# Eight input-gate tiles of the first mixer computed in quarters inside the delta-net loop

## The chip, the cores and the metric

The kernel runs on one core of a Trainium2 chip. The metric is the device time of one execution in microseconds (us); shorter is better. TensorE multiplies, VectorE (DVE), ScalarE (ACT) and GpSimd (POOL) do the elementwise work, and the SyncE queue (SP) issues the transfers of weights. All data are float32. In the trace one float32 matmul of the program leaves two TensorE records, and an identity transpose leaves one.

## The reference, cut to what matters

The program computes two transformer blocks one after the other for 256 tokens of width 1024. The part that the change touches is the end of the mixer of the first block. Two recurrent mixers (a gated delta net `dn` and an HGRN2 layer `hg`, four heads of 128 each) give one 512-wide output each. Each output goes through its own 512x1024 branch matrix, is multiplied by a sigmoid of a projection of the normed input, and the sum goes through the 1024x1024 output matrix:

```python
    def merge(parts, odn, ohg):
        br_dn = _gated_rmsnorm(odn, parts[1], dn_norm_g) @ w_br_dn
        br_hg = _gated_rmsnorm(ohg, parts[7], hg_norm_g) @ w_br_hg
        gate_dn, gate_hg = jnp.split(parts[8], 2, axis=-1)
        return (jax.nn.sigmoid(gate_dn) * br_dn + jax.nn.sigmoid(gate_hg) * br_hg) @ w_out
```

`parts[8]` is the 2048-wide gate projection of the same normed input `hx` from which all other parts come. So the gate logits do not depend on the two mixers. After this come a layer of 32 experts and the second block, which the change leaves alone.

## The kernel before, in words

**Weights.** All weights come as a stream of 1 MB blocks (`ORDER`, written by `stream_order`). SP issues them strictly in that order (`load`, L444) into a ring of slots. Up to block 48 (`EARLY`) the ring has six slots (`ring0` to `ring5`), since the other six (`ring_late`) hold intermediate values of the two mixers. Block i waits until block i-6 has been given back (`w_used`), and from block 54 on until block i-12 has. Block 54 also waits for the second `y_ready`. TensorE takes blocks in the same order (`take`) and gives them back with the increments that its matmuls carry. In the first mixer's end the blocks were: 42, 43 branch 0; 44 to 47 its gates; 48, 49 branch 1; 50 to 53 its gates; 54 to 57 the output matrix. In `merge` none of the six blocks of a branch is given back before the last gate tile of that branch (`frees` is 0 for `m2 < 3` and 5 at the first matmul of the last).

**The delta-net loop.** The delta net runs in both time directions (d = 0, 1) over four chunks s of 128 tokens. One chunk of one direction takes ten phases, and direction 1 runs four steps behind direction 0, which gives 44 steps t (`DN_SLOTS`). In phases 2 to 7 a 128x128 triangular inverse is refined: TensorE computes p (`dn_p`, four matmuls of 128 columns, one for each head), ACT copies p out of PSUM, TensorE computes x and y from it, DVE subtracts both from their operands (L1483, L1485), POOL masks a matrix for the next phase, and the next p needs DVE's and POOL's results. Phases 0, 1, 8 and 9 set up and finish a chunk. Within a step all first halves (`delta_first`) go ahead of all second halves (`delta_second`), and then comes one piece of other work (`fill_slot`): projections and transposes in steps 0 to 6, nothing from step 7 on. The four matmuls of one such product leave eight records of 128 columns.

**The end of the mixer.** After step 43 TensorE closes the output banks, ACT squares the delta-net output (`o_squares`), TensorE sums over partitions (`column_sums`), ACT takes Ln and Exp, DVE multiplies (`head_norm(1)`) and signals the second `y_ready`. Then `merge` runs eight pairs of tiles. In each pair TensorE computes a branch tile (8 matmuls of 256 columns, K = 512) and a gate tile (16 matmuls, K = 1024), ACT copies the first and takes the sigmoid of the second, and DVE multiplies, and in the second branch also adds. The last add signals `merged`, and the output product (`mix_full`, 64 matmuls) starts.

## Time and profile before

| quantity | value |
|---|---|
| time, median of 3 runs | 2779.77 us (2775.85, 2779.77, 2779.93) |
| span of the profiled execution | 2773.7 us |
| time of the profiled execution | not listed apart from its span; the lowest run is 2.2 us above the span, the median 6.1 us |
| PE busy | 2550.8 us (92%) |
| steps 7 to 43 of the delta-net loop, about | 365 to 556 us |
| from the loop's end to the second `y_ready` | 556 to 568 us |
| `merge` | 568 to 660 us |
| output product | 660 to 690 us |
| experts, loop | 745 to 1220 us |

The span runs from the first to the last instruction. A PE record's busy time has a modelled end, so the spacing from one start to the next tells how fast matmuls run. A group of the timeline view gives the start, the time it covers, the records in it and, in brackets, the idle time in front of it with the releaser. PEclk is the granted TensorE clock, where 1.0 is 2.4 GHz and 0.5 is 1.2 GHz.

### The profile page before, as it was taken

Reading aid. Unit: us, or ns where it says so; the run is one execution under the profiler, and the core shown is the slowest. Engines: PE = TensorE matmul, PEld = TensorE weight load, DVE = VectorE, ACT = ScalarE, POOL = GpSimd, SP = SyncE. Lnnn points to the kernel's source line nnn. Section 1 sums busy time; section 2 is a strip of 40 time slices with the busy share of each in tenths; the row PEclk is TensorE's granted clock in tenths of the full one; section 3 lists DMA queues with packets and bytes.
Section 4 is the critical chain, followed back from the end, with each engine's and each line's share of the span. In section 5 each row is a group of like instructions: output and inputs, shape, how many; then the busy total and the mean of one; then the engine's idle time right before and its main releaser. Section 6 shows DMA issues by size and latency. Waiting matters only on the chain.

```text
span 2773.7 us, 37722 instructions
## 1 busy us (share of the span) xinstructions
PE 2550.8 (92%) x15259; PEld 1933.4 (70%) x15264; DVE 1103.4 (40%) x2325; ACT 585.4 (21%) x1032; POOL 115.3 (4%) x98
## 2 busy tenths in 40 slices
PE   5999889989799999979999779999999997799998
PEld 2686588868456655549948468699499484586993
DVE  1455445501311111136550831366666507312665
ACT  3632422210211111121011521110100105311000
POOL 0000144300000000000000000000000000000000
PEclk8999999999999999989999889999999998799999
DMA  7126100025499999974444004344344350043340
GB/s 280 62 79 278 54 31 1 1 108 211 157 414 422 422 422 422 422 309 173 178 147 173 30 1 182 152 166 184 142 162 176 144 196 31 1 182 152 153 168 15
DMA packets 74309, 485.50 MB, mean 175 GB/s; under 512 B 7872, under 2 KB 14528, under 8 KB 16704
## 3 DMA queue, kind: packets, MB, share of 16 engines
q1 hardware_dynamic: 65808, 472.46, 42.8%
q10 hardware_dynamic: 8368, 11.14, 1.2%
q8 instruction: 98, 1.61, 0.2%
q14 instruction: 35, 0.29, 0.0%
HBM read 479.38 MB, written 4.19 MB: 174 GB/s over the span
## 4 chain that ended last, share of the span: by engine, by line
PE 82%; DVE 7%; DMA 5%; ACT 3%; issue 2%; SPq 0%; ACTq 0%; DVEq 0%; POOL 0%; POOLq 0%
PE bank L501 80%; DMA ring<-in_stream 5%; ACT arena L2010 2%; PE bank L513 2%; DVE arena L1191 1%; DVE softmax_small L1881 1%; DVE arena L1879 1%; DVE arena L1902 0%; ACT hT L2010 0%; DMA bias_scratch<-arena 0%; ACT ring_late L2010 0%; DVE arena L1449 0%; ACT L2010 0%; DVE softmax_small L1889 0%; DVE arena L1485 0%
## 5 line engine op out<-in xcount | busy, mean ns | idle before, releaser
L501 PE MATMUL bank<-arena 128*128 128x128 f32 (+4 forms) x3864 | 619.5, 318 | 67.8 <-ACT arena L2010 43.1
L501 PEld LDWEIGHTS bank<-arena 128*128 128x128 f32 (+2 forms) x3864 | 485.4, 195 | 175.5 <-issue 87.0
L501 PE MATMUL bank<-hT,ring 128*128 128x256 f32 (+2 forms) x2144 | 463.3, 374 | 8.1 <-issue 6.7
L2010 ACT ACTIVATE arena<-bank 128x512 f32<-128x512 f32 (+2 forms) x384 | 218.0, 568 | 1156.7 <-PE bank L501 1131.2
L501 PEld LDWEIGHTS bank<-hT,ring 128*128 128x128 f32 x2144 | 357.5, 193 | 97.1 <-issue 64.7
L501 PE MATMUL bank<-ring,arena 128*64 128x256 f32 (+3 forms) x2184 | 298.6, 406 | 31.3 <-DMA ring<-in_stream 29.0
L501 PE MATMUL bank<-hT,ring_late 128*128 128x256 f32 (+1 forms) x1568 | 279.4, 336 | 6.7 <-issue 6.7
L501 PEld LDWEIGHTS bank<-ring,arena 128*64 128x64 f32 (+2 forms) x2184 | 176.4, 141 | 144.7 <-issue 82.7
L501 PEld LDWEIGHTS bank<-hT,ring_late 128*128 128x128 f32 x1568 | 248.9, 193 | 31.0 <-issue 7.5
L2010 ACT ACTIVATE hT<-bank 128x256 f32<-128x256 f32 (+2 forms) x92 | 38.6, 420 | 642.4 <-PE bank L501 471.3
L501 PE MATMUL bank<-arena,ring_late 128*128 128x128 f32 (+1 forms) x1088 | 157.4, 299 | 5.1 <-DVE arena L1485 2.8
L501 PE MATMUL bank<-ring_late,hT 128*64 128x512 f32 (+2 forms) x632 | 162.0, 584 | 0.0
L1191 DVE TENSOR_TENSOR arena<-arena 128x512 f32<-128x512 f32 (+5 forms) x55 | 33.7, 615 | 321.4 <-ACT arena L2010 320.8
L501 PEld LDWEIGHTS bank<-arena,ring_late 128*128 128x128 f32 x1088 | 144.2, 193 | 12.7 <-DVE arena L1485 3.6
L513 PE MATMUL bank<-constants,arena 128*128 128x128 f32 x492 | 87.1, 325 | 58.3 <-ACT arena L2010 44.5
L501 PE MATMUL bank<-arena,ring 128*128 128x128 f32 (+1 forms) x864 | 125.0, 299 | 11.5 <-issue 8.0
L513 PEld LDWEIGHTS bank<-constants,arena 128*128 128x128 f32 x492 | 68.1, 167 | 93.1 <-issue 58.0
L1191 DVE TENSOR_TENSOR arena<-arena,bank 128x512 f32<-128x512 f32 x16 | 11.0, 688 | 303.7 <-PE bank L501 303.7
L501 PEld LDWEIGHTS bank<-arena,ring 128*128 128x128 f32 x864 | 114.1, 195 | 17.7 <-issue 12.7
L501 PEld LDWEIGHTS bank<-ring_late,hT 128*64 128x64 f32 (+1 forms) x632 | 58.1, 147 | 87.8 <-issue 85.0
L501 PE MATMUL bank<-ring_late,arena 128*64 128x256 f32 (+2 forms) x680 | 115.7, 404 | 3.2 <-DVE arena L1513 2.3
L2001 POOL TENSOR_TENSOR x_tok<-x_tok,arena 128x512 f32<-128x512 f32 x8 | 11.8, 1492 | 2207.2 <-DVE arena L1802 2207.2
(215 smaller groups left out, 2239.1 us busy)
## 6 DMA issues: line engine op xcount, KB each, us to landing
ring<-in_stream SPq DMA_DIRECT2D x248, 1024.0 KB, 8.9
ring_late<-in_stream SPq DMA_DIRECT2D x198, 1024.0 KB, 10.4
arena<-bias_scratch ACTq DMA_DIRECT2D x4, 1536.0 KB, 18.0
bias_scratch<-arena ACTq DMA_DIRECT2D x12, 256.0 KB, 2.0
constants<-in_con SPq DMA_DIRECT2D x1, 1184.0 KB, 9.3
x_tok<-in_x SPq DMA_DIRECT2D x1, 1024.0 KB, 5.3
arena<-in_ctx SPq DMA_DIRECT2D x1, 1024.0 KB, 6.8
out<-x_tok SPq DMA_DIRECT2D x2, 512.0 KB, 2.7
```

Source lines behind the costliest of these rows:

```text
L501: ins = engine.matmul(out_, lhsT, rhs, start=start, stop=stop, skip_group_check=True)
L513: ins = engine.transpose(out_, in_, ident[0:k, 0:k])
L1191: return tt(o, x, y, ALU.mult)
L1879: tt(e, src, bias2[:, m.bias], ALU.add).then_inc(*v.inc("sm_in"))
L1881: engine.tensor_reduce(stat(m, 0), e, AX.X, ALU.max).then_inc(*v.inc())
L2001: engine.tensor_tensor(x, x, ffU[j], ALU.add).then_inc(*g.inc("ff_joined"))
L2010: engine.activation(o, i, f, **kw).then_inc(*s_.inc(ev))
```

## The change

The eight gate tiles are no longer computed in `merge`. Their blocks come ahead of the branch blocks in the stream (42 to 49), those of the `hg` half first, then the branch blocks (50, 51 for `hg`; 52, 53 for `dn`), then the output matrix at 54 to 57 as before. A generator `gate_quarters` issues four matmuls of 256 columns at the end of each of the steps 7 to 38. After four quarters a tile is complete, and ACT copies it unchanged to a new place in `ring_late` (`gates1`, under slots 10 and 11) at the end of every fourth step. At steps 40 to 43 ACT takes the sigmoid of all eight tiles in place, in four passes over 1024 elements. Because `gates1` lies in slots 10 and 11, block 58 now also waits for `merged`.

After the loop the branch tiles alone are left. The branch of `hg`, whose `y_ready` is the first one, goes first. Its first tile stands ahead of `column_sums`, the other three behind it, and only then does TensorE wait for the second `y_ready`. DVE multiplies straight from PSUM with the stored gates.

```diff
--- before.py
+++ after.py
@@ -72,9 +72,8 @@
     order += qkv[0:2] + ada[0] + [("in_hg", 256 * j, "columns") for j in range(2)] + ada[1]
     order += qkv[2:3] + ada[2] + qkv[3:4] + ada[3] + qkv[4:6]
     order += [("in_z", 256 * j, "columns") for j in range(2)]
-    for b in range(2):
-        order += [(f"br{b}", 256 * j, "rows") for j in range(2)]
-        order += [("in_gate", 1024 * b + 256 * j, "columns") for j in range(4)]
+    order += [("in_gate", 1024 * b + 256 * j, "columns") for b in (1, 0) for j in range(4)]
+    order += [(f"br{b}", 256 * j, "rows") for b in (1, 0) for j in range(2)]
     order += [("out", 256 * j, "columns") for j in range(4)]
     for e in range(0, EXPERTS, 2):
         for part in ("gate", "up"):
...
@@ -343,9 +341,9 @@
         qsq, ksq = hkc, cnv
 
         a = Carve(base)
-        mrg, eg, brs = a(KT, N), [a(2, N) for _ in range(2)], [a(2, N) for _ in range(2)]
-        mtmp = a(2, N)
+        mrg, mtmp = a(KT, N), [a(2, N) for _ in range(2)]
         yx2 = a(KT, N)
+        gates1 = spare(8192, 16, N)
 
         hnZ, hnR, hnE = [None, None], [None, None], [None, None]
         hnZ[0], hnR[0], hnE[0] = hkl[0], hD[0], hX[0]
@@ -440,6 +438,8 @@
                         sp.wait_ge(sem("w_used"), i - back + 1)
                     if i == EARLY + HALF_RING:
                         sp.wait_ge(sem("y_ready"), 2)
+                    if i == EARLY + 10:
+                        sp.wait_ge(sem("merged"), 1)
                     src = A["stream"][i, :, :]
                 sp.dma_start(ring[slot][:, :], src).then_inc(sem(f"landed{slot}"), 16)
 
@@ -771,7 +771,23 @@
                     turn_tokens(v_)
                 elif t <= 6:
                     fill()
-
+                else:
+                    next(gate_pieces, None)
+
+            def gate_quarters():
+
+                for _ in range(8):
+                    w = take()[:, :].rearrange("p (m k c) -> p m k c", m=2, k=KT)
+                    t = pj_tile()
+                    for m in range(2):
+                        for k in range(KT):
+                            end = m == 1 and k == KT - 1
+                            mm(t[:, 256 * m:256 * m + 256], w[:, m, k, :], hT[:, k, LAT], start=k == 0, stop=k == KT - 1,
+                               ev="pj_full" if end else None, frees=int(end))
+                            if k % 4 == 3:
+                                yield
+
+            gate_pieces = gate_quarters()
             AB, CD = (bank[2], bank[3]), (bank[4], bank[5])
 
             def four(dst, d, f, ev=None):
@@ -865,9 +881,29 @@
                 fill_slot(t)
             clear(bank[6], stop=True)
             clear(bank[7], stop=True, ev="o_full")
-            engine.wait_ge(*pe.at("o_squared", 2))
-            column_sums([bank[3], bank[4]], flat(hnE[1]), "o_sums")
             engine.wait_ge(*pe.at("mod_read", 1))
+            engine.wait_ge(*pe.at("pj_free", state["tile"]))
+
+            def branch_tile(i, w):
+
+                if i >= 2:
+                    engine.wait_ge(*pe.at("merge_used", i - 1))
+                t = bank[i % 2]
+                for m in range(2):
+                    for k in range(4):
+                        wk = w[k // 2][:, :].rearrange("p (k c) -> p k c", k=2)
+                        c, end = 256 * (i % 4) + 128 * m, m == 1 and k == 3
+                        mm(t[:, 256 * m:256 * m + 256], wk[:, k % 2, c:c + 128], yT[1 - i // 4][:, k, :], start=k == 0,
+                           stop=k == 3, ev="branch_full" if end else None, frees=2 if end and i % 4 == 3 else 0)
+
+            for b in range(2):
+                w = [take(), take()]
+                engine.wait_ge(*pe.at("y_ready", b + 1))
+                for m2 in range(4):
+                    branch_tile(4 * b + m2, w)
+                    if b == m2 == 0:
+                        engine.wait_ge(*pe.at("o_squared", 2))
+                        column_sums([bank[3], bank[4]], flat(hnE[1]), "o_sums")
 
             def merge(branches, ys, cols, n, name="y_ready", count=None):
 
@@ -889,8 +925,6 @@
                                    stop=k == KT - 1, ev="pj_full" if k == KT - 1 and m == 1 else None,
                                    frees=0 if m2 < 3 else 5 if m == k == 0 else m == 1 and k == KT - 1)
 
-            engine.wait_ge(*pe.at("y_ready", 2))
-            merge(2, [[y[:, k, :] for k in range(4)] for y in yT], slice(NC, NC + N), 1)
             engine.wait_ge(*pe.at("merged", 1))
 
             for j in range(4):
@@ -1494,7 +1528,28 @@
                 for step in slot:
                     delta_second(step)
                 fill_slot(t)
+
+            def branch_tile(i):
+
+                engine.wait_ge(*v.at("branch_full", i + 1))
+                if i == 0:
+                    engine.wait_ge(*v.at("gates_on", 1))
+                o, g = mrg[:, 2 * (i % 4):2 * (i % 4) + 2, :], gates1[:, 2 * i:2 * i + 2, :]
+                src = bank[i % 2][:, :].rearrange("p (a b) -> p a b", a=2)
+                if i < 4:
+                    mul(o, src, g).then_inc(*v.inc("merge_used"))
+                    return
+                added = v.last()
+                mul(mtmp[i % 2], src, g).then_inc(*v.inc("merge_used"))
+                engine.wait_ge(*v.last("merge_used"))
+                engine.wait_ge(*added)
+                tt(o, o, mtmp[i % 2], ALU.add).then_inc(*v.inc("merged" if i == 7 else None))
+
+            for i in range(2):
+                branch_tile(i)
             head_norm(1, V_DNG)
+            for i in range(2, 8):
+                branch_tile(i)
 
             def merge(branches, tile, mrg, eg, brs, mtmp):
                 for b in range(branches):
@@ -1513,7 +1568,6 @@
                             tt(o, o, mtmp, ALU.add).then_inc(*v.inc("merged" if last else None))
                             engine.wait_ge(*v.last("merged" if last else None))
 
-            merge(2, TILES["merge"], mrg, eg, brs, mtmp)
             for j in range(4):
                 engine.wait_ge(*v.at("mix_full", j + 1))
                 for m in range(2):
@@ -2174,6 +2228,12 @@
                     copy_tiles([vtok[:, c].rearrange("p a b -> p (a b)") for c in range(4)])
                 elif t in (4, 6):
                     copy_tiles([hnZ[1][:, t - 4:t - 2, :]], ACT.Silu)
+                elif 7 <= t < 39 and t % 4 == 2:
+                    i = (t - 10) // 4
+                    copy_tiles([gates1[:, 2 * i:2 * i + 2, :]])
+                elif 40 <= t < 44:
+                    i = 4 * (t - 40)
+                    act(gates1[:, i:i + 4, :], gates1[:, i:i + 4, :], ACT.Sigmoid, "gates_on" if t == 43 else None)
 
             of = lambda x, d: x[:, 4 * d:4 * d + 4, :]
             ps = lambda i: bank[i][:, :].rearrange("p (a b) -> p a b", a=4)
@@ -2225,8 +2285,6 @@
                         copy_tiles([brs[i % 2]])
                         t = tile()
                         act(eg[i % 2], t[:, :].rearrange("p (a b) -> p a b", a=2), ACT.Sigmoid, "pj_free")
-
-            merge(2, 0, eg, brs)
 
             def norm(name, first, junk=None):
 
```

On TensorE, steps 14 to 18 of the loop. In the kernel before, with the segment product (`ring_late,constants`) that begins a chunk of direction 1, one transpose set (`L513`), and the x and y products behind them:

```order
L501 MATMUL bank<-ring_late,constants 128x512
L501 MATMUL bank<-arena 128x128 x16
L513 MATMUL bank<-constants,arena 128x128 x4
L501 MATMUL bank<-arena 128x128 x52
L501 MATMUL bank<-arena,ring_late 128x128 x4
L501 MATMUL bank<-ring_late,arena 128x128 x4
```

The same place in the kernel after, where `hT,ring` are the quarters:

```order
L501 MATMUL bank<-ring_late,constants 128x512
L501 MATMUL bank<-arena 128x128 x12
L501 MATMUL bank<-hT,ring 128x256 x4
L501 MATMUL bank<-arena 128x128 x4
L513 MATMUL bank<-constants,arena 128x128 x4
L501 MATMUL bank<-arena 128x128 x8
L501 MATMUL bank<-hT,ring 128x256 x4
L501 MATMUL bank<-arena 128x128 x24
L501 MATMUL bank<-hT,ring 128x256 x4
L501 MATMUL bank<-arena 128x128 x20
```

Each step now ends with four matmuls of 256 columns, just ahead of the first product of the next step. Nothing stands between the first and the second half of a step that did not stand there before.

On TensorE behind the loop, before (first rows of eight pairs):

```order
L501 MATMUL bank<-zero 128x512 x2
L501 MATMUL bank<-arena,ones 128x512 x2
L501 MATMUL bank<-arena,ring 128x256 x8
L501 MATMUL bank<-hT,ring 128x256 x16
L501 MATMUL bank<-arena,ring 128x256 x8
L501 MATMUL bank<-hT,ring 128x256 x16
```

And after, down to the output product:

```order
L501 MATMUL bank<-zero 128x512 x2
L501 MATMUL bank<-arena,ring 128x256 x8
L501 MATMUL bank<-arena,ones 128x512 x2
L501 MATMUL bank<-arena,ring 128x256 x56
L501 MATMUL bank<-arena,ring_late 128x256 x64
```

The 128 gate matmuls are gone from here, and one branch tile stands ahead of the column sums (`arena,ones`).

On ACT, the end of the loop after (copies of the delta net, sigmoids over `ring_late`, the two squares in the last row of two, then Ln and Exp):

```order
L2064 ACTIVATE arena<-bank 128x512 x2
L2064 ACT_TABLE_LOAD
L2064 ACTIVATE ring_late<-ring_late 128x1024
L2064 ACTIVATE arena<-bank 128x512
L2064 ACTIVATE ring_late<-ring_late 128x1024
L2064 ACTIVATE arena<-bank 128x512 x2
L2064 ACTIVATE ring_late<-ring_late 128x1024 x2
L2064 ACTIVATE arena<-bank 128x512 x2
L2064 ACT_TABLE_LOAD
```

The table load for the sigmoid stood behind the loop, in `merge`, and now stands at step 40; neither the copies nor the squares between it and the Ln have a load of their own.

## Rows read from the trace of the kernel before

**Rows 1.** The page: busy time by engine, with share and number of records.

```profile
PE 2550.8 (92%) x15259; PEld 1933.4 (70%) x15264; DVE 1103.4 (40%) x2325; ACT 585.4 (21%) x1032; POOL 115.3 (4%) x98
```

**Rows 2.** Windows view: loop, a slow stretch in it, and the experts.

```profile
core 0: us, PE busy (x) PEld busy (x) DVE busy (x) ACT busy (x) POOL busy (x), PEclk, DMA share, GB/s
365.00:557.00 192.00, 172.88 (x1401) 162.56 (x1401) 103.43 (x160) 48.99 (x81) 78.55 (x63) 0.99 0.02 7
412.00:414.00 2.00, 2.00 (x11) 2.00 (x11) 0.00 (x0) 0.60 (x1) 2.00 (x3) 0.50 0.00 0
...
763.00:1200.00 437.00, 434.64 (x3103) 258.59 (x3102) 58.31 (x195) 78.76 (x120) 0.00 (x0) 1.00 1.01 421
```

**Rows 3.** Waits view, 365 to 557 us: us in total, times, longest.

```profile
PE bank L501 <- ACT arena L2010: 8.7, 12, 0.9
PE bank L501 <- DVE arena L1483: 4.7, 4, 3.0
```

**Rows 4.** Timeline of PE in the loop, 364 to 560 us.

```profile
373.55 2.05 PE L501 MATMUL bank<-arena 128*128 128x128 f32 x16 [0.75 <-ACT arena L2010]
...
410.12 11.81 PE L501 MATMUL bank<-arena 128*128 128x128 f32 x88 [2.96 <-DVE arena L1483]
...
444.34 1.16 PE L501 MATMUL bank<-arena,ring_late 128*128 128x128 f32 x8 [1.02 <-DVE arena L1485]
...
464.61 10.30 PE L501 MATMUL bank<-arena 128*128 128x128 f32 x88 [1.19 <-DVE arena L1483]
...
553.90 2.05 PE L501 MATMUL bank<-arena 128*128 128x128 f32 x16 [0.78 <-DVE arena L1489]
```

**Rows 5.** Timeline of all engines behind the loop, 548 to 720 us.

```profile
556.00 0.38 PE L501 MATMUL bank<-zero 128*128 128x512 bf16 x1
...
557.76 1.98 PE L501 MATMUL bank<-arena,ones 128*128 128x512 f32 x4 [1.38 <-ACT arena L2010]
...
563.84 1.06 ACT L2010 ACTIVATE arena<-arena 128x1024 f32<-128x1024 f32 x1
...
567.76 5.55 PE L501 MATMUL bank<-arena,ring 128*128 128x256 f32 x16 [8.02 <-issue]
...
580.05 3.62 PE L501 MATMUL bank<-arena,ring 128*128 128x256 f32 x16
580.29 1.28 ACT L2010 ACT_TABLE_LOAD   x1 [6.27 <-PE bank L501]
581.59 0.60 ACT L2010 ACTIVATE arena<-bank 128x512 f32<-128x512 f32 x1
...
583.50 7.07 PE L501 MATMUL bank<-hT,ring 128*128 128x256 f32 x32
...
590.41 3.62 PE L501 MATMUL bank<-arena,ring 128*128 128x256 f32 x16
...
614.77 5.38 PE L501 MATMUL bank<-arena,ring 128*128 128x256 f32 x16 [3.48 <-DMA ring<-in_stream]
...
651.07 7.07 PE L501 MATMUL bank<-hT,ring 128*128 128x256 f32 x32
...
658.23 0.60 ACT L2010 ACTIVATE arena<-bank 128x512 f32<-128x512 f32 x1 [6.29 <-PE bank L501]
...
658.93 0.69 DVE L1191 TENSOR_TENSOR arena<-arena 128x512 f32<-128x512 f32 x1 [8.94 <-ACT arena L2010]
...
660.41 29.49 PE L501 MATMUL bank<-arena,ring_late 128*128 128x256 f32 x128 [2.27 <-DVE arena L1513]
```

**Rows 6.** Tile view of `ring`, 600 to 640 us: issue to landing of six blocks.

```profile
DMA to landing us min/median/max: 4.8/8.0/12.7
```

**Rows 7.** Timeline of ACT near the loop's end, 540 to 590 us.

```profile
543.56 0.60 ACT L2010 ACTIVATE arena<-bank 128x512 f32<-128x512 f32 x1 [3.31 <-PE bank L501]
547.46 0.60 ACT L2010 ACTIVATE arena<-bank 128x512 f32<-128x512 f32 x1 [3.31 <-PE bank L501]
```

More of the change, by code:

```diff
@@ L139 @@
             ("ada2", 1), ("hg", 2), ("ada3", 1), ("dk1", 2), ("ada4", 1), ("dk", 2), ("ada5", 1), ("dv0", 2), ("osum", 2),
-            ("qsum", 2), ("ktok", 4), ("dv", 2), ("ada", 2), ("z0", 1), ("vtok", 4), ("z", 1))
+            ("qsum", 2), ("ktok", 4), ("dv", 2), ("ada", 2), ("z0", 1), ("vtok", 4), ("z", 1), ("gates", 8))
 TILES = {name: sum(n for _, n in S1_TILES[:i + 1]) for i, (name, _) in enumerate(S1_TILES)}
-TILES["merge"] = TILES["z"]
-TILES["h2"] = TILES["merge"] + 16 + 4
+TILES["h2"] = TILES["gates"] + 4
 TILES["layers"] = TILES["h2"] + 14
```

## Prediction, made before the changed kernel ran

> **What bounds the kernel now.** I read the page first: TensorE (PE) is busy for 2550.8 us of 2773.7 [rows 1], so a change pays only where PE has less to do, waits less, or runs at the higher clock. The change touches two stretches, and I read each with the windows view, then the waits, then the timeline.
>
> The first is the delta-net loop from step 7 on, 365 to 557 us. PE is busy for 172.9 of 192 us there at a granted clock of 0.99 [rows 2], so 19.1 us are idle. The waits view splits them: 8.7 us in 12 waits on ACT (x waits for ACT's copy of p, in the middle of a step), 4.7 us in four waits on DVE's L1483 [rows 3], the rest in small ones. The timeline shows both kinds. A row such as 373.55 with 0.75 is the first kind and recurs. The wait of 2.96 at 410.12, 1.19 at 464.61 and 1.02 at 444.34 (and the same again ten steps later, at 499.55) are the second: the first products of a step wait for DVE [rows 4]. Everywhere else PE runs without a gap: 88 records in 10.30 us [rows 4].
>
> The second stretch runs from the closing of the output banks at 556.00 to the output product at 660.41, so 104.4 us [rows 5]. In it the reader is to see: 8.02 us idle while ACT and DVE turn the column sums into the second `y_ready`; eight pairs of tiles, a branch tile taking 583.50 - 580.05 = 3.45 us and a gate tile 590.41 - 583.50 = 6.91 us; 3.48 us idle for a transfer at 614.77, since the blocks of the second branch can be fetched only when the first branch gives its own back; and two branch tiles of 5.55 and 5.38 us instead of 3.62, each behind an idle time [rows 5].
>
> **What is added to the loop.** 32 quarters make up the eight gate tiles, so PE gets 8 x 6.91 = 55.3 us more work there, 1.73 us in each of 32 steps. A quarter stands at the end of a step. It can hide only in a wait of the first products of the next step, not in the 8.7 us of waits on ACT, which lie between the halves. Of the 19.1 us idle, 10.4 are not on ACT. The 2.96 wait exceeds a quarter by 1.2, and the steps 39 to 43 have no quarter; there two waits of 0.78 on DVE remain (553.90 is one [rows 4]). That leaves 7.6 us. The printed idle time leaves out the modelled tail of the record before it (a wait printed as 0.75 is 0.91 by start-to-start spacing), and summing the starts record by record I get 9.2 us for steps 8 to 38. I take 9. There is a second saving. Behind the 2.96 wait the granted clock is 0.50 [rows 2], which is 1.2 GHz, and 88 records take 11.81 us instead of 10.30 [rows 4], 1.5 more. With a quarter in that wait, and another 1.73 us before it in which DVE's work of the previous step is already under way, less than 1 us of idle is left, and I expect the fall to go. ACT's eight copies of the tiles (0.60 each) mostly end before the next p is done; in three places a transpose set of half a product's length leads the step and its copy starts some 0.1 us late, 0.3 us together. The loop costs 55.3 - 9 - 1.5 + 0.3 = 45.1 us. The bounds are 55.3 + 0.3 (nothing hidden) and 55.3 - 19.1 - 1.5 = 34.7 (all idle time filled); I stay near the record-by-record sum, since place by place it says which waits lie in front of a step.
>
> The sigmoids: four passes of 1.06 us (the Exp over 1024 elements at 563.84 is the nearest row [rows 5]) and a table load of 1.28. From the end of one copy to the next, 544.16 to 547.46, ACT has 3.3 us [rows 7]; load and pass need 2.4. The others need 1.1 each and end near 555, ahead of the squares. I cost them at nothing; uncovered they would be 4 x 1.06 + 1.28 = 5.5 us. On the load the trace has 1.28 us and the next pass starts at 581.59, 1.30 after it [rows 5]. The Trainium skill (ScalarE: Activation LUTs, What ACT_TABLE_LOAD costs) counts a drain besides and gives about 2.66 us for each switch. By that, load and pass would take 3.7 us and PE would lose 0.4 us once; by the row it loses nothing, and I go by the row.
>
> **What is left behind the loop.** The banks are closed at 556.2. Then 8 x 3.45 = 27.6 us of branch tiles and 4 x 0.43 = 1.7 us of column sums (four records of 512 columns, each twice the 0.216 of 256) bring PE to 585.5. Is PE kept going? The sums end at 556.2 + 3.45 + 1.7 = 561.4 instead of 559.5, so the second `y_ready` comes 1.9 us later, at 569.6 instead of 567.7. The fourth branch tile ends at 571.7, 2.1 us after it. DVE has multiplied tiles 0 and 1 before `head_norm(1)` and does tile 2 at 570.3, so the bank for tile 4 is free at 571.7 as well. From the last record to the output product it took 660.41 - (651.07 + 6.91) = 2.43 us; ACT's pass between them (658.23 to 658.93, 0.70) goes [rows 5], so 1.73 remain. The output product starts at 587.3 instead of 660.41, 73.1 us less: 55.3 of gate tiles moved, 9.7 of idle time around the norm (8.02 + 1.38, and drains), 1.9 + 1.8 of low clock, 3.5 of transfer wait and 0.7 of ACT.
>
> SP: blocks 54 to 57 wait for the second `y_ready` and are issued at 569.6 and in the 1.5 us behind it. Blocks fetched six at a time landed 4.8 to 12.7 us after issue [rows 6], so the last is there by 584 and the first long before, ahead of 587.3. Block 58 and all behind it wait for `merged` at 587; the first expert block is needed some 84 us later, and twelve blocks at 421 GB/s [rows 2] take 30 us. Cost nothing.
>
> **Sum.** -73.1 + 45.1 = -28.0 us. The profiled execution spans 2773.7 us, which gives 2745.7. Its own time is not listed; the median of the three runs lies 6.1 us above the span, and I keep that distance: 2751.8, rounded to 2752. The output product ran its first records at the low clock behind a wait of 2.27 us (29.49 us where 128 x 0.216 = 27.6 would do [rows 5]); I leave that 1.8 in, and it may go.
>
> **Rivals.**
> - *The waits move along.* DVE's work behind a step starts when PE's products end, and what a quarter hides may come back in the next wait. For it: the waits at 410.12 and 464.61 both name DVE's L1483 as what ended last [rows 4], and DVE's chain there is some 9 us long. Against: that chain starts from products ahead of the quarter, not from the quarter. If nothing is hidden and the slow stretch stays, the loop costs 55.6 and the sum is -17.5: 2762.
> - *More is hidden than the places allow.* POOL and DVE run ahead by 1.7 us in each step, and the waits in the middle shrink too. Then the loop costs 34.7 and the output product loses its slow start: -73.1 + 34.7 - 1.8 = -40.2: 2740. Against: the 0.75 of the wait at 373.55 is the time from PE's own p through ACT's copy, which no quarter shortens [rows 4].
> - *The output weights come late.* If blocks 54 to 57 took twice the 12.7 us, the last would land near 597 and the product would start some 6 us late and again wait between blocks; with a slow stretch behind it (1.8) about 8 us in all: 2760. Against: rows 6 and a free queue.
> - *Slower than before: the clock.* If PE, denser now, were granted 1.2 GHz in parts of the loop, each us of work there would take two. Losing more than 28 us needs 28 us of work at half clock, 56 us or a quarter of the 237 us from step 7 on: 2780 and above. Against: 434.6 busy us of 437 in the experts ran at 1.00, and the fall at 412 follows idle time, not density [rows 2, 4].
>
> **How the numbers follow.** Forecast 2752: 0.74 (its own range 2746 to 2757). Waits move along, 2762: 0.11. More hidden, 2740: 0.08. Late weights, 2760: 0.04. Slower, by the clock or a wait I have not seen: 0.03. The range 2743 to 2762 leaves out about half of the second rival's, a part of the first's and the slower case. A measurement of this kernel tells 0.2% (5.6 us) from no change. Faster 0.95, same 0.02, slower 0.03.
>
> **What would show it.** In the profile after: quarters as `hT,ring` groups of eight records, 1.73 us, at the end of 32 steps; the loop from step 7 to the closed banks some 236 us instead of 191; the wait of 2.96 gone or under 1 us and no clock below 1.0 there; 31 us from the closed banks to the output product, with no wait longer than 0.5 us among the branch tiles; the output blocks landed before it. If the waits on ACT in the loop grow well past 8.7 us or the loop takes over 242 us, the first rival holds. If PE waits for `ring_late` ahead of the output product, the third does.

## The result and the profile after

The changed kernel takes 2745.72 us (median of 4 runs, 2743.99 to 2747.15) against 2777.81 us (4 runs, 2773.29 to 2779.93) for the kernel before on the same chip. The ratio is 0.9891, with a 95% interval of 0.9879 to 0.9903. The forecast was 2752 us with a range of 2743 to 2762, and faster at 0.95. The span went from 2773.7 to 2744.8 us, that is -28.9 us where the sum said -28.0.

The same landmarks, read from TensorE's timeline, order all kernels of this study. All times are us from the start of the span.

| landmark | before | after | difference |
|---|---|---|---|
| step 7 begins | 365.4 | 365.9 | +0.5 |
| output banks closed, step 43 done | 556.2 | 599.8 | +43.6 |
| output product begins | 660.4 | 630.8 | -29.6 |
| transposes of the next norm begin | 691.1 | 659.9 | -31.2 |
| experts begin | 744.8 | 715.2 | -29.6 |
| span | 2773.7 | 2744.8 | -28.9 |

Timeline of PE after, in the loop and at its end. The rows at 370.50 and 375.81 answer to 373.55 of [rows 4], 422.14 to 410.12, 597.45 to 553.90.

```profile
370.50 1.89 PE L501 MATMUL bank<-hT,ring 128*128 128x256 f32 x8
...
375.81 2.05 PE L501 MATMUL bank<-arena 128*128 128x128 f32 x16 [0.75 <-ACT arena L2064]
...
422.14 5.71 PE L501 MATMUL bank<-arena 128*128 128x128 f32 x48 [0.79 <-DVE arena L1517]
...
597.45 2.05 PE L501 MATMUL bank<-arena 128*128 128x128 f32 x16 [0.78 <-DVE arena L1523]
599.34 0.59 PE L501 MATMUL bank<-zero 128*128 128x512 bf16 x2
599.77 3.62 PE L501 MATMUL bank<-arena,ring 128*128 128x256 f32 x16
603.22 1.88 PE L501 MATMUL bank<-arena,ones 128*128 128x512 f32 x4
604.94 24.34 PE L501 MATMUL bank<-arena,ring 128*128 128x256 f32 x112
...
630.79 27.89 PE L501 MATMUL bank<-arena,ring_late 128*128 128x256 f32 x128 [1.51 <-DVE arena L1546]
```

The first row is a quarter: eight records of 256 columns, and 1.73 us to the next group. One quarter now stands in the wait of 2.96 us for DVE and another one step ahead of it, and 0.79 is left. The mid-step wait of 0.75 for ACT's copy is as it was. Behind the loop there is one branch tile, the column sums, and seven more tiles in 24.34 us without a gap, where before eight pairs, 8.02 us of idle and a 3.48 us wait stood [rows 5].

Windows after: the loop, the place that answers to the slow stretch of [rows 2] (behind the wait at 422.14), the stretch up to the output product, and the experts.

```profile
core 0: us, PE busy (x) PEld busy (x) DVE busy (x) ACT busy (x) POOL busy (x), PEclk, DMA share, GB/s
365.00:596.00 231.00, 220.32 (x1639) 206.17 (x1639) 98.12 (x159) 56.28 (x91) 76.66 (x63) 1.00 0.10 33
423.00:426.00 3.00, 3.00 (x28) 2.96 (x27) 0.69 (x1) 1.19 (x2) 2.65 (x3) 1.00 0.00 0
596.00:631.00 35.00, 32.71 (x157) 27.75 (x157) 11.69 (x18) 9.94 (x11) 0.00 (x0) 1.00 0.31 121
733.00:1170.00 437.00, 435.24 (x3111) 259.16 (x3109) 58.30 (x195) 78.73 (x120) 0.00 (x0) 1.00 1.01 421
```

The granted clock is 1.00, that is 2.4 GHz, throughout the loop and up to the output product, and the experts are what they were. Waits of PE after, 365 to 601 us (us in total, times, longest), which answer to [rows 3]:

```profile
PE bank L501 <- ACT arena L2064: 9.0, 13, 0.9
PE bank L501 <- DVE arena L1517: 0.8, 1, 0.8
PE bank L501 <- DVE arena L1519: 0.8, 1, 0.8
PE bank L501 <- DVE arena L1523: 0.8, 1, 0.8
```

The 4.7 us on DVE have become 0.8, and the 8.7 us on ACT are still there, at 9.0. ACT's timeline after shows the sigmoids:

```profile
587.11 0.60 ACT L2064 ACTIVATE arena<-bank 128x512 f32<-128x512 f32 x1 [3.31 <-PE bank L501]
587.72 1.28 ACT L2064 ACT_TABLE_LOAD   x1
589.01 1.06 ACT L2064 ACTIVATE ring_late<-ring_late 128x1024 f32<-128x1024 f32 x1
591.01 0.60 ACT L2064 ACTIVATE arena<-bank 128x512 f32<-128x512 f32 x1 [0.94 <-PE bank L501]
```

The load takes 1.28 us, begins 0.01 after the copy before it and the pass follows at once; ACT then waits 0.94 us for PE, not PE for ACT.

### The profile page after: what moved, and what is told of

It reads as the page before. It is cut to its first block, busy times and chain, and to the rows that moved or that the text cites. A ratio compares the mean times of both kernels' runs of the same rounds, so it can differ in the third digit from the quotient of the medians.

```text
span 2744.8 us, 37714 instructions
## 1 busy us (share of the span) xinstructions
PE 2544.3 (93%) x15264; PEld 1928.8 (70%) x15264; DVE 1099.4 (40%) x2325; ACT 584.5 (21%) x1028; POOL 113.4 (4%) x98
## 4 chain that ended last, share of the span: by engine, by line
PE 84%; DVE 6%; DMA 4%; ACT 3%; issue 2%; SPq 0%; ACTq 0%; DVEq 0%
PE bank L501 82%; DMA ring<-in_stream 3%; ACT arena L2064 2%; PE bank L513 2%; DVE softmax_small L1935 1%; DVE arena L1933 1%; DVE arena L1956 1%; DVE arena L1225 1%; ACT hT L2064 0%; ACT ring_late L2064 0%; DMA bias_scratch<-arena 0%; ACT L2064 0%; DVE softmax_small L1943 0%; DVE arena L1930 0%; ACT small L2064 0%
## 5 line engine op out<-in xcount | busy, mean ns | idle before, releaser
L2064 ACT ACTIVATE arena<-bank 128x512 f32<-128x512 f32 (+1 forms) x368 | 208.3, 566 | 1080.3 <-PE bank L501 1056.1
L513 PE MATMUL bank<-constants,arena 128*128 128x128 f32 x492 | 87.7, 327 | 57.4 <-ACT arena L2064 43.4
L513 PEld LDWEIGHTS bank<-constants,arena 128*128 128x128 f32 x492 | 68.2, 168 | 92.2 <-issue 58.3
L1225 DVE TENSOR_TENSOR arena<-arena 128x512 f32<-128x512 f32 (+5 forms) x47 | 26.0, 556 | 237.1 <-ACT arena L2064 236.5
```

Of the source, the lines that this page charges most:

```text
L513: ins = engine.transpose(out_, in_, ident[0:k, 0:k])
L1225: return tt(o, x, y, ALU.mult)
L2064: engine.activation(o, i, f, **kw).then_inc(*s_.inc(ev))
```

## Experiments

**The theory.** The gain is the sum of two things with places of their own. (a) Gate work fills PE's waits, those in front of a step in the loop, about 12 us with the slow stretch. (b) What PE waited for behind the loop (the norm of the delta-net output, the weights of the second branch) is covered by branch tiles that need neither. **The rival** is that one of the two does it all, or that moving the work pays by the order of weights alone. The first two kernels undo one part each. Each ratio is to the kernel before on the same chip. Its median was 2776.12 us beside kernels 1 to 4, 2776.53 beside 5 to 7 and 2775.24 beside 8, against 2777.81 beside the changed kernel, so a difference of medians between kernels of two such groups is good to a us or two. Step 7 also begins at other times, from 363.0 us (kernel 2) to 365.9 (the changed kernel), ahead of anything that differs on TensorE between them; so the loop is measured from there.

**1. The gate tiles behind the loop.** The quarters leave the loop, and so do ACT's copies and sigmoids. All eight gate tiles are computed behind it, one ahead of the column sums, and the branch tiles follow them.

```diff
-                else:
-                    next(gate_pieces, None)
...
+            for _ in range(4):
+                next(gate_pieces, None)
+            engine.wait_ge(*pe.at("o_squared", 2))
+            column_sums([bank[3], bank[4]], flat(hnE[1]), "o_sums")
+            for _ in gate_pieces:
+                pass
```

> The changed kernel with no gate tile in the loop: all eight are computed behind it, one ahead of the column sums and seven behind them, then the eight branch tiles; stream, buffers and the give-back of each block as in the changed kernel. Theory (the loop hides part of the gate tiles in its waits in front of a step, and all of the rest of the gain comes from the stretch behind the loop): steps 7 to 43 go back from 233.9 us to 190.8, the stretch behind takes 55.3 us more without a wait of its own, so +12.3 us against the changed kernel, about 2758 us, with the wait of 2.96 us and the slow stretch behind it back. Rival (the loop hides nothing, its length comes from elsewhere; the gate tiles cost the same wherever they stand once the chain to the second y_ready is covered): within 2 us of the changed kernel, 2744 to 2748.

Measured: 2757.70 us (2756.35 to 2758.57), ratio 0.9932 (0.9918 to 0.9945), span 2754.4. Waits of PE in its loop, 365 to 557 us:

```profile
PE bank L501 <- ACT arena L2063: 8.6, 12, 0.9
PE bank L501 <- DVE arena L1518: 4.7, 4, 3.0
```

The waits of the kernel before are back, to a tenth of a us. The low clock behind the longest of them is not:

```profile
410.57 10.30 PE L501 MATMUL bank<-arena 128*128 128x128 f32 x88 [2.96 <-DVE arena L1518]
```

Its loop takes 189.3 us (365.82 to 555.16), which is the 190.8 of the kernel before less 1.5 of slow stretch. With the quarters in it the loop takes 233.9, so 44.5 us were paid for 55.3 us of work and 10.8 are hidden. The output product begins at 642.46, 11.7 us later than after the change: these 10.8, and a wait of 0.79 us in front of the first branch tile, which the change does not have. The expected 12.3 had the slow stretch in it. What is won behind the loop stays.

**2. The branch tiles behind the norm.** The quarters stay in the loop, but the column sums go first and all eight branch tiles wait for the second `y_ready`.

```diff
+            engine.wait_ge(*pe.at("o_squared", 2))
+            column_sums([bank[3], bank[4]], flat(hnE[1]), "o_sums")
...
+            engine.wait_ge(*pe.at("y_ready", 2))
...
-                    if b == m2 == 0:
-                        engine.wait_ge(*pe.at("o_squared", 2))
-                        column_sums([bank[3], bank[4]], flat(hnE[1]), "o_sums")
```

> The changed kernel with the column sums first and all eight branch tiles behind the second y_ready, as before the change; the quarters stay in the loop. Theory (the branch tiles that need only the first y_ready cover the chain of squares, sums, Ln, Exp and DVE): PE waits some 1.4 us for the squares and 8.0 us for the second y_ready, and the first branch tile behind them runs at the low clock for 1.9 us more, so the stretch from the closed banks to the output product takes 42 to 43 us instead of 31.0 and the kernel 11 to 12 us more, about 2757 us. Rival (the chain is only pushed back by the tiles ahead of it, so their order is worth little): +2 us or less, up to 2748.

Measured: 2758.19 us (2756.09 to 2759.59), ratio 0.9934 (0.9921 to 0.9948), span 2754.1. Its timeline of PE behind the loop:

```profile
596.43 0.60 PE L501 MATMUL bank<-zero 128*128 128x512 bf16 x2
598.40 1.99 PE L501 MATMUL bank<-arena,ones 128*128 128x512 f32 x4 [1.37 <-ACT arena L2061]
608.52 30.28 PE L501 MATMUL bank<-arena,ring 128*128 128x256 f32 x128 [8.13 <-issue]
```

The 8.13 us are the 8.02 of [rows 5] again, and the 128 records behind them take 30.28 us where 128 x 0.216 = 27.6 would do: the granted clock was 0.50 for 10.2 us from 603.2, after the idle time began. From the closed banks (596.86) to the output product (640.31) it takes 43.5 us instead of 31.0, half a us above the 42 to 43 expected, so the order of the tiles is worth 12.4. The product begins only 9.5 us later than after, because step 7 had begun 2.9 us earlier, at 363.01. The loop takes 233.85 us, as after the change. Both parts are real: 10.8 us in the loop, 12.4 behind it, and about 12 us each on the medians. Neither kernel waits for a transfer among its branch tiles, so that part of the gain does not hang on what covers the norm; it comes with the new order of the blocks, and kernel 5 prices it.

**3. Quarters in the middle of steps.** The 9.0 us of waits on ACT lie between the halves of a step. Ten quarters moved there should take most of them away. Steps 8 to 11, 19, 20, 29 and 30 have a full wait (0.75 or 0.87), steps 21 and 31 a smaller one; the full waits of steps 39 to 41 are left alone.

```diff
+GATE_AT = [(7, 1), (8, 0), (9, 0), (10, 0), (11, 0), (12, 1), ...]
...
+                for _ in range(GATE_MID[t]):
+                    next(gate_pieces)
```

> The changed kernel with ten of the 32 quarters (steps 8 to 11, 19 to 21, 29 to 31) moved from the end of their step to its middle, between the first and the second halves, where PE waits for ACT's copy. Theory (a quarter hides in the wait that stands right behind its place and in no other): the waits of 0.91 us by start-to-start spacing at 375.8, 382.1, 389.4, 395.3, 445.6, 452.8, 514.5 and 521.6 us and two of 0.3 to 0.5 go, 7 to 8 us less in the loop, about 2738 us. Rival (the step is bound by its chain from p over ACT, x, y and DVE to the next p, so a later x brings the wait back in front of the next step): no change within 1.5 us, 2744 to 2747.

Measured: 2737.46 us (2735.61 to 2739.12), ratio 0.9858 (0.9843 to 0.9873), span 2735.9. PE's timeline in step 8 of this kernel, at the place that answers to 375.81 above:

```profile
373.35 1.06 PE L506 MATMUL bank<-arena 128*128 128x128 f32 x8
374.24 1.89 PE L506 MATMUL bank<-hT,ring 128*128 128x256 f32 x8
375.97 1.95 PE L506 MATMUL bank<-arena 128*128 128x128 f32 x16
```

The quarter stands between p and what needs p's copy, and the wait of 0.75 is gone. The waits on ACT in the loop are 2.6 us in 4 instead of 9.0 in 13, the banks are closed at 591.4 instead of 599.8, and the product begins at 622.45. From step 7 (365.25) the loop takes 226.2 us instead of 233.9, 7.7 less where 7 to 8 were expected.

**4. Waits first.** The quarters stand where PE was seen to wait, up to step 42, and two at a time where it is long: 14 in the middle of steps, 18 at an end. The lines taken out below are those of kernel 3.

```diff
-GATE_AT = [(7, 1), (8, 0), (9, 0), (10, 0), (11, 0), (12, 1), ...]
+GATE_AT = [(8, 0), (9, 0), (10, 0), (11, 0), (11, 1), (12, 1), (13, 1), (14, 1), (15, 0), (15, 1), (15, 1), (19, 0), ...,
+           (37, 1), (39, 0), (40, 0), (41, 0), (41, 1), (42, 1)]
```

> The same 32 quarters placed by where PE was seen to wait: 14 in the middle of steps 8 to 11, 15, 19 to 21, 29 to 31, 39 to 41, and 18 at the ends of steps 11 to 14, 15 (two), 21, 22, 24, 25, 31, 32, 34 to 37, 41, 42; none in the full steps 16 to 18, 23, 26 to 28, 33, 38. Theory (a quarter hides in the wait behind its place): 8.7 us of waits in the middle of steps up to 31, 1.0 at step 16, and 4.6 of the 4.9 us in steps 39 to 43 go, 13 to 14 us less, about 2732 us. Rival (the single-direction steps 39 to 43 are a chain in which a quarter costs its full 1.73 us, and the waits of the middle move to the next step's start): 2742 to 2747.

Measured: 2730.90 us (2729.35 to 2731.06), ratio 0.9834 (0.9821 to 0.9847), span 2728.5. The one wait of PE in the loop that its waits view lists is this:

```profile
PE bank L506 <- DVE arena L1524: 0.2, 1, 0.2
```

The banks are closed at 583.5, 16.3 us earlier than after, with the same work done. Of these, 1.0 lies ahead of step 7 (364.90). The loop takes 218.6 us, 15.2 less than after, where 13 to 14 were expected.

**5. The transfer wait by itself.** This is the kernel before, with one thing changed: the first four blocks of the second branch lie in the free late slots, so that they can be fetched ahead. It prices the 3.5 us of transfer wait and the low clock behind it in my term for the second stretch.

```diff
+    if i < EARLY + 4:
+        return i % RING + HALF_RING, 1
+    if EARLY + HALF_RING <= i < EARLY + HALF_RING + 4:
+        return i % RING - HALF_RING, EARLY // HALF_RING + 1
...
-                    back = HALF_RING if i < EARLY + HALF_RING else RING
+                    back = HALF_RING if i < EARLY or i in (52, 53, 60, 61, 62, 63) else RING
```

> The kernel before with one thing changed: blocks 48 to 51 (the second branch and its first two gate blocks) go into slots 6 to 9, free from the second y_ready on, and so are fetched while the first branch is computed; 54 to 57 take slots 0 to 3 instead. Theory (the second branch waited for its transfer because the first gave its blocks back late, and the idle time then cost TensorE its clock): the wait of 3.5 us at 614.8 us goes and the branch tile behind it takes 3.45 us instead of about 5.3, so 5.3 us less from the second y_ready to the output product (87.4 us instead of 92.7), about 2771 us beside a before of 2776. Rival (the low clock behind the wait is not its consequence): 3.5 us less, and 1.8 us of low clock at the same place or the next.

Measured: 2778.43 us (2776.47 to 2780.16, 11 runs) against 2776.53 (15 runs), ratio 1.0005 (0.9996 to 1.0014), span 2776.6. The expectation of 2771 us failed. Yet the wait is gone, and PE reached the norm at 683.48 instead of 691.07, 7.6 us earlier. Of these, 5.7 lie between the closed banks and the output product (98.4 us instead of 104.2), 1.6 in the product, which ran without its slow start (27.89 us instead of 29.49), and 0.3 ahead of step 7. Its experts begin at 747.04 instead of 744.84: between the two landmarks it lost 9.8 us. ACT's waits in its router, 700 to 735 us, and windows of ten microseconds in which the router's bias rows are written, first in this kernel and then in the kernel before:

```profile
ACT arena L2014 <- DMA bias_scratch<-arena: 15.1, 9, 7.0
```

```profile
708.00:718.00 10.00, 3.02 (x5) 0.73 (x5) 6.01 (x28) 2.01 (x4) 0.00 (x0) 0.63 1.01 416
```

```profile
714.00:724.00 10.00, 8.64 (x14) 2.84 (x14) 5.69 (x26) 4.40 (x8) 0.00 (x0) 0.83 0.42 159
```

The router writes twelve bias rows to memory from ACT's queue, and ACT may reuse a row buffer only when its write has landed. In this kernel the DMA engines are full at that moment (share 1.01, 416 GB/s against 159), one write takes 10.0 us instead of 2.0, ACT stands behind the writes for 15.1 us (5.9 before) and PE has 3.0 busy us of 10. The transfers in the way are expert blocks. SP issues in order, and blocks 60 to 63 wait for slots that the output weights now hold. Block 63 and the six behind it, 64 to 69, were issued from 699.7 to 703.3; the slots of these six had long been free (kernel 8 fills them from 645.8 to 655.3). In the kernel before a single block was left at that point, at 705.8. The Trainium skill (DMA: Bandwidth & Descriptors, Issuing engines are not separate DMA queues) says that transfers issued from different engines run on the same 16 DMA engines and interleave there. The 10.0 us of a write from ACT beside blocks from SP agree.

**6. The sigmoid at each copy.** The gates are not kept raw: each copy is a sigmoid, which ACT can do straight from PSUM, and the four passes go.

```diff
-                    copy_tiles([gates1[:, 2 * i:2 * i + 2, :]])
-                elif 40 <= t < 44:
-                    i = 4 * (t - 40)
-                    act(gates1[:, i:i + 4, :], gates1[:, i:i + 4, :], ACT.Sigmoid, "gates_on" if t == 43 else None)
+                    copy_tiles([gates1[:, 2 * i:2 * i + 2, :]], ACT.Sigmoid)
```

> The changed kernel with the sigmoid taken at each of the eight copies out of PSUM, and no copy kept raw and no pass later. Each of them needs a table load of 1.28 us, and the next Exp another. Theory (ACT's copy of p stands right behind the gate tile's copy in its queue, and x and y wait for it): in each of the eight steps behind a copy the copy of p comes some 1 us later and PE waits that much in the middle of the step, 7 to 11 us in all, 2753 to 2757 us. Rival (ACT is busy for a quarter of the loop only, so the loads are hidden): within 1.5 us of the changed kernel, 2744 to 2747.

Measured: 2753.32 us (2752.86 to 2754.99), ratio 0.9919 (0.9905 to 0.9932), span 2751.3. The groups of ACT in its loop, 365 to 606 us (count, busy us, mean ns, idle before), and one place where PE waits behind a load:

```profile
L2064 ACT ACT_TABLE_LOAD x14 | 18.0, 1283 | 45.8 <-PE bank L501 45.8
```

```profile
391.76 1.28 ACT L2064 ACT_TABLE_LOAD   x1 [3.92 <-PE bank L501]
393.06 0.60 ACT L2064 ACTIVATE ring_late<-bank 128x512 f32<-128x512 f32 x1
393.68 1.23 ACT L2064 ACTIVATE arena<-bank 128x512 f32<-128x512 f32 x2
```

```profile
394.96 1.56 PE L501 MATMUL bank<-arena 128*128 128x128 f32 x8 [1.95 <-ACT arena L2064]
396.31 3.21 PE L501 MATMUL bank<-hT,ring 128*128 128x256 f32 x8
```

Fourteen loads stand there, seven ahead of a gate's pass and seven ahead of a pass from PSUM that the code has as an Exp; after the change there are two between 365 and 604 us, one of each kind. The load and the gate's own pass stand ahead of the copy of p, and the wait of 0.75 becomes 1.95; the quarter behind it ran at the low clock, 3.21 us instead of 1.89. The waits on ACT are 15.3 us instead of 9.0. From step 7 (364.39) to the closed banks (606.00) it takes 241.6 us, 7.8 more than after, within the 7 to 11 expected: 6.3 of them are the longer waits, and the rest, 1.5, is about what the low clock of 395.6 to 399.0 costs. To keep the gates raw is worth 6 us, and the 7.6 of the medians with that slow stretch.

**7. Waits first, and an early output product.** Kernel 4, whose output product starts as soon as six of the eight feature tiles are merged.

```diff
-            engine.wait_ge(*pe.at("merged", 1))
+            engine.wait_ge(*pe.at("merge_most", 1))
...
+                        if j == m == 0 and k == 6:
+                            engine.wait_ge(*pe.at("merged", 1))
```

> The kernel with the quarters placed by the waits, and besides the output product starts on the first six of its eight feature tiles before the last merged pair is there. Theory (1.5 us of wait ahead of the output product, against 2.6 us of matmuls that do not need the last pair): the wait goes, 1.5 us less in the trace between the closed banks and the end of the output product, about 2729 us against 2731, which the times can hardly tell. Rival (the early matmuls only move the wait to the seventh): nothing in the trace either.

Measured: 2727.05 us (2726.34 to 2728.44), ratio 0.9825 (0.9811 to 0.9838), span 2725.2. Timeline of PE in kernel 4 and then in this one:

```profile
614.53 27.89 PE L506 MATMUL bank<-arena,ring_late 128*128 128x256 f32 x128 [1.51 <-DVE arena L1553]
643.59 1.97 PE L518 MATMUL bank<-constants,arena 128*128 128x128 f32 x16 [1.17 <-DVE arena L1582]
```

```profile
612.89 27.79 PE L506 MATMUL bank<-arena,ring_late 128*128 128x256 f32 x128
641.85 1.97 PE L518 MATMUL bank<-constants,arena 128*128 128x128 f32 x16 [1.17 <-DVE arena L1584]
```

The wait of 1.51 is gone and the product begins 1.6 us earlier, as expected. The experts begin 3.0 us earlier (696.0 against 699.0): the other 1.3 us lie in the norm and the router, 54.2 us instead of 55.4 long, where the low clock fell on other matmuls. That part is luck of the place, and it can go again. The span is 3.3 us shorter, where the expectation was 1.5. It is the fastest kernel of the study, 49.5 us under the kernel before.

**8. The missed kernel with its refill reordered.** Kernel 5, and SP issues the six expert blocks whose slots come free first ahead of the four that must wait longer.

```diff
-                    load(i, place(i)[0])
+                    j = (66, 67, 68, 69, 64, 65, 60, 61, 62, 63)[i - 60] if 60 <= i < 70 else i
+                    load(j, place(j)[0])
```

> The kernel before with the second branch's first weights loaded ahead, as in the run before this one, which missed: there PE no longer waited 3.48 us at 614 and reached the norm at 683.5 instead of 691.1, and the 7.6 us were lost again in the router. The only edit against that kernel: SP issues the first expert blocks in another order. Six blocks whose ring slots are free before the output product ends (66 to 69, 64, 65) go ahead of four whose slots come free one by one with the output product (60 to 63). Theory: in the missed run eight blocks stood behind the four on SP's in-order queue, were issued from 699.7 to 703, and were still landing (DMA share 1.02 from 710 to 720) when ACT wrote the router's bias rows; a write took up to 10.0 us instead of 2.0 and ACT stood 15.1 us behind such writes instead of 5.9. With one to three blocks left there, as in the kernel before (two at 705.8), the router takes its 53.8 us from norm to experts again, so the experts start at 737 to 739 instead of 747.0, the idle time of ACT behind the writes is about 6, and the time is 2768 to 2772, ratio 0.997 to 0.9985. Rival: the low clock in the norm and the router (34 of 60 us in the missed run) is the cause, brought on by the short idle before them, and the writes only ride on it; then the order of the loads changes nothing and the time is 2777 to 2779, ratio 1.000. Slower, 2785 and more, if a block of the experts is now late.

Measured: 2769.92 us (2767.39 to 2770.92, 11 runs) against 2775.24 (15 runs), ratio 0.9980 (0.9971 to 0.9989), span 2767.9. The windows view of ten microseconds of its router, and ACT's waits there:

```profile
708.00:718.00 10.00, 9.55 (x16) 2.78 (x15) 4.90 (x21) 4.24 (x8) 0.00 (x0) 0.83 0.51 191
```

```profile
ACT arena L2015 <- DMA bias_scratch<-arena: 7.3, 9, 1.1
```

PE reaches the norm at 683.61, as in kernel 5, and the experts begin at 738.01 instead of 747.04. The time is within the 2768 to 2772 expected. (The expectation counts eight blocks in the way in kernel 5 and two in the kernel before; by the packets in the traces from there to the experts, 1008 and 144 at 144 for each block, it was seven and one.) Only the order of the transfers was changed, and from norm to experts it takes 54.4 us instead of 63.6. So most of the missing gain of kernel 5 had been lost to transfers that landed on top of the bias writes. Of the 9.2 us, 1.6 lie ahead of the first bias product (703.22), where a stretch of low clock had begun at 690.0, before those blocks were issued; no run ties that part to them. Kernel 8 keeps 5.3 us on the median and 7.5 up to the norm, and part of that is luck: 1.5 in the loop, where the slow stretch at 411 did not come, and 1.6 in the output product, which had no slow start. From the closed banks to the product it gains only 4.3 us, since its first branch tile ran longer at the low clock (6.45 us against 5.38). The wait itself, by the starts in kernel 5 against those before, is worth 3.6 us and the clock behind it 1.8, together the 5.3 expected to 0.1.

## Why the prediction was right

| term of the sum | predicted | measured |
|---|---|---|
| start to step 7 | 0 | +0.5 |
| quarters in the loop | +55.3 | 8 records each, spacing 1.73: +55.3 |
| hidden, less ACT's copies | -8.7 | -10.8 (by kernel 1) |
| slow stretch in the loop | -1.5 | -1.5 |
| loop, step 7 to closed banks | +45.1 | +43.0 (233.85 against 190.84) |
| closed banks to output product | -73.1 | -73.2 (31.0 against 104.2) |
| slow start of the output product | 0, "may go" | -1.6 (27.89 against 29.49) |
| behind the output product | 0 | +2.3 |
| span | -28.0 | -28.9 |

*The quarters.* The waits in front of a step took them, and those in the middle of one did not, as argued: 4.7 us on DVE's product went to 0.8, and ACT's 8.7 stayed at 9.0. Kernel 1 shows that this is worth 10.8 us, kernels 3 and 4 that the middle waits were open to a quarter placed there. Hidden was 2.1 us more than I gave it. The rival "more is hidden" is not the reason, for it wanted the middle waits to shrink. Setting the 1401 other records of the loop in kernel 1 beside those after, start by start, 10.7 us are gone, and all but a few tenths of it at the first products of steps 12 to 36. Of the 2.1, 0.4 is the long wait, which left 0.79 where I had 1.2. The rest must lie in pauses of 0.1 to 0.5 us at the start of a step, most of them too short for the rows; my record-by-record sum does not list them, so which ones it had too low stays open. The printed idle time fell by 7.0 us, from 18.5 to 11.5 in the loop; my 19.1 had taken in 0.6 us behind the closed banks. Printed idle time understates the pauses, so 34.7 was no lower bound either: kernel 4's loop costs 27.8 us more than the one before.

*The slow stretch.* No clock below 1.0 is left from step 7 to the output product. But kernels 1 and 8 have the same wait of 2.96 us and run the 88 records behind it in 10.30 us, at full clock, and kernel 8 has the loop of the kernel before unchanged. So the fall at 411 did not have to follow from that wait. That the term of 1.5 us came out is in part luck.

*Behind the loop.* The best term of all, -73.2 against -73.1. The second `y_ready` comes at 613.0, and PE first asks for it behind the fourth tile at 599.8 + 3.45 + 1.7 + 3 x 3.45 = 615.3, 2.3 us later; I had said 2.1. Kernel 2 shows what stands there when nothing covers it: 8.13 and 1.37 us of idle time and a low clock, 12.4 us in all. Start by start in the trace before, the 17.9 us by which 73.2 exceeds the 55.3 of moved work are 11.7 of this kind (9.8 idle and 1.9 of low clock), 5.4 of transfer wait with its clock, and 0.8 that the last step to the output product is shorter; the last no run measures by itself.

*Transfers.* The output weights were issued from 613.11 to 614.43 and landed 4.8 to 10.9 us after issue, the last before 630.8. The rival of late weights is out. Kernels 5 and 8 price the transfer wait: the 3.5 us and the low clock behind it were well sized up to the output product, but a gain there by itself is kept only if the later transfers stay clear of the router. After the change they do: SP issues six expert blocks from 632.3 on and the last that the ring has room for at 675.9, ahead of the bias writes, whose median time to landing is 2.0 us as before.

*The sigmoids.* Hidden, as costed. Kernel 6 shows the price when they are not gathered. The Trainium skill (ScalarE: Activation LUTs, What ACT_TABLE_LOAD costs) would add a drain to the load and have cost PE 0.4 us once. The trace does not agree: 0.01 us lies between the copy's end and the load's start, and the pass begins 1.29 us after the load does.

*The slower rival.* PE at 220 busy us of 231 was granted 1.00 all through the loop. In kernel 4 it was 218.4 of 218.6, at 1.00 too. Density did not lower the clock.

*What was off.* The slow start of the product went, which I left open. It came back behind it: between the norm at 659.9 and the experts at 715.2 the windows show a clock of 0.70 and 0.82 where before it was 0.89 and 0.87, and this part took 55.4 us instead of 53.8.

```profile
659.00:676.00 17.00, 9.62 (x54) 8.60 (x54) 6.38 (x14) 8.58 (x16) 0.00 (x0) 0.70 0.33 119
676.00:715.00 39.00, 28.68 (x114) 17.01 (x113) 16.80 (x75) 10.28 (x19) 0.00 (x0) 0.82 0.29 108
```

From the experts on, 0.7 us more were lost over 2029 us, which no row explains. And most of the 6 us between 2752 and the measured median is not in the sum: I carried the 6.1 us between the span of one execution and the median of the first three runs, while the profiled execution after stands at 2746.74, 1.9 us above its span of 2744.8, and later executions of the kernel before, each with its own span, stand 1.7 to 2.8 above it. Two slips of the working change nothing: the parts listed for 73.1 add up to 72.9, and 104.4 counts from 556.00 where the sum uses 556.2.

## What to carry to other kernels

Filler work pays twice if it is cut to the size of the waits and put in front of the instruction that waits. The same eight tiles hid 10.8 us at the ends of steps, and the time fell by 14.8 us more once the pieces followed the list of waits, 7.7 of it by ten pieces moved between a product and the use of its copy. A wait list with releasers tells which of the two places a filler can reach. Work that depends on nothing late belongs behind the last thing that a late result depends on, here three tiles behind the column sums, and one ahead of them for the wait on the squares. When a stall is removed early in a chain and the total stays, look at what the moved transfers meet: the order on one in-order queue decided here whether most of 7.6 us was kept.

## What the runs showed of the hardware

- A small write shares the DMA engines with whatever else is in flight. A 256 KB write of bias rows took 2.0 us beside a share of 0.4 and up to 10.0 us beside a share of 1.01.
- Stretches of 1.2 GHz were seen, from step 7 to the experts, in or behind stretches in which PE idled, but not behind every wait: the 2.96 us wait near 410 had one in the kernel before (from 411.1) and in kernel 5 (from 410.2), and none in kernels 1 and 8, all with the same loop. So where they fall differs between kernels that do the same there, and a difference of 1 to 3 us between two kernels may be no more than that.
- One and the same DVE instruction took 0.69 us in some executions and 1.8 in others, and the long ones are those beside work of GpSimd. It is L1449 in the kernel before and L1483 after; L1487 (L1453 before) belongs to the same phase. VectorE groups, first before (365 to 557 us), then after (365 to 600 us):

```profile
L1449 DVE TENSOR_TENSOR arena<-constants,arena 128x512 f32<-128x512 f32 x6 | 7.5, 1242 | 0.2
```

```profile
L1487 DVE TENSOR_TENSOR arena<-constants,arena 128x512 f32<-128x512 f32 x6 | 9.8, 1641 | 0.2
L1483 DVE TENSOR_TENSOR arena<-constants,arena 128x512 f32<-128x512 f32 x6 | 4.2, 692 | 0.2
```

Before, GpSimd is idle during three of the six executions of L1449, and these take 0.69 us; it works during the other three, and these take 1.78 to 1.80. After, it is idle during all six, and all six take 0.69. It works beside each of the six of L1487, which take 1.64. It is not so for every form: instructions that read a PSUM bank took 0.67 to 0.69 us beside GpSimd too, and so did most of those from the arena and the constants at L1191. No run changed GpSimd's work alone, so why some forms are slowed is open.
